# Where the first group of each head drains its banks, and how the last norm scales and stores its rows

## What is computed

```python
def hybrid_layer(h, w_in, conv_w, a_log, dt_bias, dn_norm_w, w_out, pos):
    proj = h @ w_in
    ...
    qkv = jax.nn.silu(causal_depthwise_conv(jnp.concatenate([aq, ak, av], axis=-1), conv_w))
    ...
    o_a = gated_delta_chunked(q_a, k_a, v_a, beta, g)      # has a triangular solve
    ...
    o_b = dilated_attention(q_b, k_b, v_b)
    ...
    return jnp.concatenate([y_a, y_b], axis=-1) @ w_out

x = x + g2 * (jnp.square(jax.nn.relu(h2 @ w_ff1)) @ w_ff2)
return rms_norm(x, norm_final_g)     # x * rsqrt(mean(x*x) + EPS) * g
```

## Time and profile before

| | us |
|---|---|
| median of 3 runs | 2894.06 |
| lowest and highest of these | 2893.16, 2895.57 |
| the profiled execution | 2890.94 |
| its span, first to last instruction | 2889.2 |
| first looped head: PE starts its second group at | 121.43 of the span |
| OUTA: PE starts its second group at | 721.12 of the span |
| last norm: PE starts its sums at | 2876.43 of the span |

### The profile page before, as it was taken

The page is one execution under the profiler, slowest core; times in us unless marked ns, Lnnn a source line. Parts: engine busy times, 40 slices in busy tenths (PEclk is TensorE's granted clock), DMA queues, the critical chain, the costliest instruction groups (busy, mean ns, idle before and its releaser), DMA issues.

```text
span 2889.2 us, 51927 instructions
## 1 busy us (share of the span) xinstructions
PE 2839.9 (98%) x17818; PEld 2521.2 (87%) x17818; DVE 2143.4 (74%) x3130; ACT 1484.7 (51%) x2140; POOL 452.5 (16%) x188
## 2 busy tenths in 40 slices
PE   7999999999999999999999999999999999999998
PEld 6888888888888888888897999988888888888887
DVE  7777777777679888888887899987786446565456
ACT  4454444444344444444445788865545444444443
POOL 0111101111000000000000000000004445455453
PEclk9999999999999999999999999999999999999999
DMA  6544444545568888788886777766775567667555
GB/s 235 170 151 150 160 157 158 165 162 174 162 211 306 308 298 314 281 318 305 302 287 209 221 239 238 231 207 236 282 286 175 194 214 242 230 232 251 199 183 181
DMA packets 211197, 651.81 MB, mean 226 GB/s; under 512 B 34552, under 2 KB 54392, under 8 KB 210304
## 3 DMA queue, kind: packets, MB, share of 16 engines
q1 hardware_dynamic: 177120, 616.61, 61.9%
q10 hardware_dynamic: 33952, 33.52, 3.7%
HBM read 626.95 MB, written 23.09 MB: 225 GB/s over the span
## 4 chain that ended last, share of the span: by engine, by line
PE 65%; issue 25%; DVE 5%; ACT 3%; DMA 1%; DVEq 0%; ACTq 0%; SPq 0%; POOL 0%; POOLq 0%
PE gemm L626 39%; PE gemm L630 20%; DVE wl L1697 2%; ACT wh L1101 1%; PE gemm L623 1%; PE gemm L624 1%; DVE dT L1895 1%; DVE dW L1893 1%; DMA raw<-in_stream 1%; DVE gB L1915 0%; ACT gA L1211 0%; DVE cb L1702 0%; ACT gB L1204 0%; PE side L761 0%; PE side L783 0%
## 5 line engine op out<-in xcount | busy, mean ns | idle before, releaser
L1101 ACT ACTIVATE wh<-raw 128x1024 fp32r<-128x1024 f32 x939 | 983.1, 1058 | 934.5 <-PE gemm L630 811.2
L626 PE MATMUL gemm<-xs,wh 128*128 128x512 f32 x4320 | 1363.7, 397 | 10.0 <-DVE cb L1702 3.4
L1697 DVE TENSOR_TENSOR wl<-raw,wh 128x1024 fp32r<-128x1024 f32 x811 | 1033.9, 1280 | 426.3 <-ACT wh L1101 404.5
L630 PEld LDWEIGHTS gemm<-xs,wl 128*128 128x128 f32 x5088 | 927.9, 188 | 180.7
L630 PE MATMUL gemm<-xs,wl 128*128 128x256 f32 x5088 | 1004.8, 279 | 0.0
L626 PEld LDWEIGHTS gemm<-xs,wh 128*128 128x128 f32 x4320 | 656.7, 188 | 21.4 <-DVE cb L1702 7.4
L626 PE MATMUL gemm<-hid,wh 128*128 128x512 f32 x2112 | 664.5, 396 | 4.7 <-DVE xacc L1717 2.3
L630 PEld LDWEIGHTS gemm<-hid,wl 128*128 128x128 f32 x2368 | 436.0, 188 | 90.4
L630 PE MATMUL gemm<-hid,wl 128*128 128x256 f32 x2368 | 467.3, 279 | 0.0
L1625 POOL TENSOR_TENSOR wl<-raw,wh 128x1024 fp32r<-128x1024 f32 x128 | 348.1, 2724 | 362.4 <-ACT wh L1101 361.1
L626 PEld LDWEIGHTS gemm<-hid,wh 128*128 128x128 f32 x2112 | 318.4, 188 | 7.4 <-issue 2.8
(11 more groups left out here) (416 smaller groups left out, 2132.0 us busy)
## 6 DMA issues: line engine op xcount, KB each, us to landing
raw<-in_stream SPq DMA_DIRECT2D x940, 512.0 KB, 4.2
ada_a<-in_ada SPq DMA_DIRECT2D x144, 512.0 KB, 5.0
ada_b<-in_ada SPq DMA_DIRECT2D x48, 512.0 KB, 4.9
parts_scratch<-parts SPq DMA_DIRECT2D x28, 256.0 KB, 4.0
pairs<-parts_scratch SPq DMA_DIRECT2D x112, 64.0 KB, 3.6
stash<-stage ACTq DMA_DIRECT2D x12, 512.0 KB, 4.5
att<-stash ACTq DMA_DIRECT2D x8, 384.0 KB, 5.2
x<-in_x SPq DMA_DIRECT2D x4, 512.0 KB, 5.7
```

Source lines behind the costliest of these rows:

```text
L626: mm(G[n][:, :], w, moving, start=first, stop=False, skip_group_check=True)
L630: op = mm(G[n][:, 0:T] if whole else G[n][:, T:2 * T], wl[:, slot, at:at + P], rhs(sl * SLAB_K + k)[:, 0:T], start=False, stop=last, skip_ ...
L1101: A(wh[:, slot, :], raw[:, slot, :], ACT.Copy).then_inc(hi_ready, 1)
L1697: tt(wl[:, slot, :], raw[:, slot, :], wh[:, slot, :].bitcast(F32), ALU.subtract).then_inc(lo_ready[slot], 1)
```

## The change

Two parts are independent of each other.

In the heads, the tail of group gi 0 moves on DVE. For h = 1 to 7 both halves are called at place 0 of step 6, ahead of the split of that step, that is ahead of the low part of slab 9 (slab 1 of the next group). Before, banks 0 and 1 were added at place 0 of step 7 and banks 2 and 3 at place 2 of step 7. For the first group of OUTA banks 0 and 1 are drained at place 0 of step 6 and banks 2 and 3 at place 0 of step 7. The hook of slot 12 stays where it is, behind the split of step 6. ACT, PE, POOL and SP run the same order as before in this part.

In the last norm, ACT multiplies x by `final2` in place (16 operations of 128 x 256): those of group i - 1 at hooks 1, 3, 5 and 7 of group i, those of the last group behind its squares. DVE then multiplies by the factor alone, in five operations over 2, 3, 4, 4 and 3 rows of tiles, each with its store by SP.

```diff
+    weighted = loads["x0"]
...
-                    if tail is not None and sl == nslabs - 1 and tail_at[half] == place:
+                    if tail is not None and (sl, place) == (
+                            tail_at[half] if isinstance(tail_at[half], tuple) else (nslabs - 1, tail_at[half])):
                         tail(half)
...
+    HEADS_AHEAD, OUTA_AHEAD = ((6, 0), (6, 0)), ((6, 0), (7, 0))
...
+    OUT_PARTS = [(0, 2), (2, 5), (5, 9), (9, 13), (13, 16)]
...
-        for k in range(4):
-            sp.wait_ge(S("out_ready"), k + 1)
-            sp.dma_start(out_d[:, 4 * k:4 * k + 4, :], x[:, 4 * k:4 * k + 4, :]).then_inc(S("out_stored"), 16)
-        sp.wait_ge(S("out_stored"), 64)
+        for part, (k0, k1) in enumerate(OUT_PARTS):
+            sp.wait_ge(S("out_ready"), part + 1)
+            sp.dma_start(out_d[:, k0:k1, :], x[:, k0:k1, :]).then_inc(S("out_stored"), 16)
+        sp.wait_ge(S("out_stored"), 16 * len(OUT_PARTS))
...
+        def weights(i, j):
+
+            k = 4 * i + j
+            act.wait_ge(norm_sq, SQ_AT[4] + (i + 1 if i < 3 else 4 + j))
+            A(x[:, k, :], x[:, k, :], ACT.Copy, scale=V("final2", k, 1)).then_inc(weighted, 1)
+
         for i in range(4):
-            walk(Q_FF + 16 * (FF_QUARTERS - 1) + 8 + 2 * i, 8, split)
+            def hook(slot):
+                if i > 0 and slot in (1, 3, 5, 7):
+                    weights(i - 1, slot // 2)
+            walk(Q_FF + 16 * (FF_QUARTERS - 1) + 8 + 2 * i, 8, split, hook)
             squares(4, i)
+        for j in range(4):
+            weights(3, j)
...
-                walk(6 * h + 2 * gi, 8, split, hook, 16 * gi, POOL_NONE, tail=out, tail_at=HEADS_DVE,
+                walk(6 * h + 2 * gi, 8, split, hook, 16 * gi, POOL_NONE, tail=out,
+                     tail_at=HEADS_AHEAD if gi == 0 and not isinstance(h, int) else HEADS_DVE,
                      ahead=ahead if gi == 0 else None)
...
-                 tail_at=HEADS_DVE if gi < 3 else INTO_X)
+                 tail_at=OUTA_AHEAD if gi == 0 else HEADS_DVE if gi < 3 else INTO_X)
...
-        for q in range(4):
-            for j in range(4):
-                k = 4 * q + j
-                op = stt(x[:, k, :], x[:, k, :], V("final2", k, 1), ps1[:, 0:T], ALU.mult, ALU.mult)
-            op.then_inc(S("out_ready"), 1)
+        for k0, k1 in OUT_PARTS:
+            dve.wait_ge(weighted, LOADED + k1)
+            tt(x[:, k0:k1, :], x[:, k0:k1, :], ps1[:, 0:T].unsqueeze(1).to_broadcast([P, k1 - k0, T]), ALU.mult
+               ).then_inc(S("out_ready"), 1)
```

## The result

The changed kernel takes 2914.07 us, the kernel before 2893.61 us (medians of six runs each). The ratio is 1.0084 (95% interval 1.0069 to 1.0100): slower by 0.8%, where no change was forecast. Its runs also spread more, 2912.59 to 2929.61 us. (Of all runs in this text one, of the kernel with low part 9 on POOL, took 5726 us; it is in no ratio.) The profiled execution has a span of 2912.0 us, 22.8 us more than before, and PE's granted clock falls from 0.998 to 0.993 on average.

What follows compares the result with a forecast made beforehand. PE, busy 98% of the span, was taken as the bound, with the load of `Em` behind DVE's chain limiting gains in the heads. Heads +1.2 and end -1.4 gave -0.2 us, so 2893.9 us, range 2889.3 to 2900.0.

Steps and rivals of the forecast that it cites:

- PE's 1.16 us at the banks: Loop heads: PE's loss of 1.16 us a head, waiting for DVE's bank additions between groups, goes.
- OUTA's boundary: OUTA's first group: PE loses 2.3 us before, about 1.6 us after; gain 0.65 us.
- the end's sum: Last norm: five multiplications take 4.64 us, last store lands at 2887.35 against 2888.74; gain 1.4 us.
- The upper bound: Heads: all seven at the longest landing of `Em`, +9.6 us.
- rival C: Heads: DMAs collide, `Em` takes 6.8 us in all heads; +8.2 us in all, 2902.3 us; chance 0.17.
- the first term: Heads with OUTA: banks' gain turns into a wait for `Em`, whose chain comes 1.22 us later; sum +1.2 us.
- `Em` is issued at 214.35: Second looped head: copy, both stores and load of `Em` all come 1.22 us later, load issued at 214.35 against 213.13.
- SP's refill behind it (slab 13) is issued 2.5 us later than now ... I cost it at nothing: Heads: refill behind low part 9 goes 2.5 us later; PE needs that slab some 11 us later, so no cost.
- ACT loses little: Heads, slot 18: ACT's next conversion is due at about 211.7, the copy it waits for ends at 212.0.
- A head's period: Loop heads, sign of being right: period within 0.5 us of what it was.
- B: Heads: DVE's limit decides as `Em` lands quicker; heads -2.9, end -1.4, 2889.8 us; chance 0.17.
- D: Heads: neither limit is real, DVE makes up the delay elsewhere; -10.2 us, 2883.9 us; chance 0.08.

Runs made afterwards that it cites:

- `fill`: Changed kernel with four idle PE products of 128 x 256 words ahead of the wait for `Em` in each of eight heads; 2913.42 us (1.0085).
- `end_only`: Kernel before with only the change's part in the last norm; 2891.40 us (0.9998).
- `heads_only`: Kernel before with only the change's part in the heads, last norm as before; 2921.43 us (1.0092).

## Why the prediction was wrong

**Right.** PE's 1.16 us at the banks went; low part 9 was in time; the copy came 1.20 us later (1.22); line 765 became the new wait in most heads, here all; DVE's 4.64 us were 4.68 and the end gained 1.37 us of 1.4. OUTA's boundary loses 1.4 us, 0.9 less than before (0.65 forecast). Two terms of the end's sum, 0.7 us from the first issue to the first byte and 0.5 us from the last byte to the landing, stood in no row; the trace has 0.8 and 0.3. The upper bound and rival C's +9.6 are 7 x 1.44 - 0.5, printed as 7 x 1.4 - 0.5.

**Wrong, the first term.** The step that failed reads "`Em` is issued at 214.35": it shifted the chain copy, stores, load by 1.22 us and kept the stores' landing as it was. No row had suggested that it could grow, because in the kernel before the stores fall into a lull of the DMAs (shares of 0.28 and 0.35), and I bounded the load of `Em` (4.8 to 6.8 us) but put no bound on the stores ahead of it. There was a hint in the earlier trace rows: a load of 256 KB took 5.4 us, where the page's median for a refill of 512 KB is 4.2, so these DMAs on ACT's queue were slower for their size. The stores took 2.7 to 6.2 us instead of 1.9. The step beside it, "SP's refill behind it (slab 13) is issued 2.5 us later than now ... I cost it at nothing", is the cause: I checked that the slab would be in time, not what its transfer would run beside. For the second head: 3.6 us more for the store, 1.2 us less for the load (4.5 instead of 5.7). "ACT loses little" failed with it: ACT waits for the stores' landing itself and starts the conversion behind it only at 219.48, after 4.9 us idle; with slabs three ahead PE's waits for low parts stay at 0.6 us in all. A head's period, which was to stay within 0.5 us, grew by 1.1 to 4.0 us.

**Wrong, the second term.** The prediction left out the clock. After waits of 3.5 to 4.0 us the granted clock is at the lower of its two levels, 1.2 GHz. The second looped head of the changed kernel (last columns: granted clock, DMA share, GB/s):

```profile
222.00:224.00 2.00, 1.06 (x5) 1.07 (x6) 1.81 (x5) 0.00 (x0) 0.00 (x0) 0.50 0.87 252
224.00:226.00 2.00, 2.00 (x9) 1.81 (x9) 1.57 (x2) 0.00 (x0) 0.00 (x0) 0.50 0.35 131
226.00:228.00 2.00, 2.00 (x10) 1.81 (x8) 0.00 (x0) 0.39 (x1) 0.00 (x0) 0.50 0.74 262
228.00:230.00 2.00, 2.00 (x13) 1.83 (x13) 1.02 (x3) 0.67 (x1) 0.00 (x0) 0.86 0.00 0
```

From the start of `Em`'s products to the first bank product behind `Dm`'s it took 3.08 us before (219.71 to 222.79), and 3.42, 5.81, 3.20, 5.69, 4.77, 4.80, 3.75 and 3.17 us in the eight heads after: 10.0 us more in sum, 8.8 of it in the four heads whose wait was 2.4 us or longer. In these four the granted clock is below 1 in the windows behind the wait; in the other four it is 1.00. `fill` shows the price from the other side. The Trainium skill, TensorE: Matmul & The Clock Gate, "What's actually happening", tells of a clock that falls when TensorE idles; the trace agrees. The prediction left it out, though its own forecast had waits up to 2.6 us.

The sum closes up to OUTA. At `Em`'s product in OUTA the changed kernel is 755.52 - 734.71 = 20.8 us behind. Waits for `Em` 19.9, less 0.3 that the kernel before had, less 7 x 1.16 and 0.9 at the banks, plus 10.0: 20.6 us. Between there and the last norm another 3.4 us are lost, in the second block, which the change leaves alone; no run tells whether that is more than spread (`end_only` is 1.6 us sooner there than the kernel before).

**The rivals.** C had the sign and half of the mechanism (the same DMAs collide) but the wrong victim: the load, which was slow already and got no slower, instead of the stores. Its price of +8.2 us came from the load's longest landing alone, and its chance of 0.17 was too low. B and D are refuted as told for this kernel, but B's number, 2889.8, and the gain it stood for are within reach: with the additions one place later the kernel is at 2886.

That the refills are the cause is shown from both sides: removed one by one (1.9 from up to 6.2 us), put into the kernel before (3.3 to 3.8 from 1.9), and left in place under a later chain (1.9). Not settled is why the store took about 3.3 us in three loop heads and 4.2 or more in the other four.

## What to carry to other kernels

When a step on one engine frees a buffer that a DMA queue refills, moving the step moves the transfer: look up which small, latency-bound DMAs it will now run beside, not only whether the slab comes in time. Put bounds on every link of a chain through memory, also on those that look constant, since a row of 1.9 us may only tell of a lull. Drain banks early, but behind the low part that releases a refill, not ahead of it; and price a wait of TensorE of several microseconds with the half clock behind it.

## What the runs showed of the hardware

A 32 KB store lands in 1.9 us with few other transfers in flight, in 3.3 to 3.8 us with a 512 KB load issued 0.2 us ahead, and in up to 6.2 us among several; a 32 KB load took 5.0 us instead of 1.9 with a 512 KB load issued 0.07 us behind it, while the 256 KB load into `Em` took 3.2 to 7.3 us over all kernels. A POOL operation on 128 x 1024 words (2.4 us) beside a DVE operation with two inputs lengthened the latter by 2.1 us in both cases seen (3.35 from 1.22, 2.34 from 0.20). In the changed kernel PE's products behind waits of 1.3 to 1.9 us kept to 1.1 to 1.2 us, and behind the four waits of 2.4 to 4.0 us the granted clock fell for some microseconds. The border is not sharp: in `heads_only` it fell behind a wait of 1.96 us and not behind waits of 2.07 and 2.26 us.
